# Two layers of a hybrid token mixer and MoE: norm and modulation in the transposed layout, projection by stream, alternating heads and halving sums

## The reference, cut

```
def trunk_layer(x, cvec, lw, gla_s0, k_ctx, v_ctx):
    sh1, sc1, g1, sh2, sc2, g2 = ada_mod(cvec, lw['w_ada'], lw['b_ada'])      # silu(c) @ w_ada + b_ada, in six
    h = rms_norm(x, lw['norm_mix']) * (1 + sc1) + sh1
    gq, gk, gv, gg, glr, conv_in, nq, nk, nv = jnp.split(h @ lw['w_in'], split_points, axis=-1)
    gla_o, gla_state = gla_mixer(...)                                         # gated linear attention, both directions
    conv_o = conv_module(...)
    na = attend_dense(q, k, v)  or  neighborhood_attention(q, k, v, k_ctx, v_ctx, lw['na_rpb'])
    mix = jnp.concatenate([gla_o, conv_o, from_heads(na)], axis=-1) @ lw['w_out']
    x = x + g1 * mix
    h = rms_norm(x, lw['norm_ffn']) * (1 + sc2) + sh2
    x = x + g2 * moe(h, ...)          # sigmoid router, top 8 of 64 experts within 4 of 8 groups, one shared expert
```

## Time and profile before

| | |
|---|---|
| median of 3 runs | 1586.37 us (1584.79 to 1589.13) |
| the profiled execution | 1593.01 us, its span 1591.3 us |
| mean granted TensorE clock | 0.966 of full |
| busy in the span | PE 92%, PEld 49%, DVE 29%, ACT 16%, POOL 7% |
| costliest group, expert matmuls L939 on `ring` | 375.4 us busy, 25.5 us of waits, 15.0 of them for loads |
| loads of expert weights | 3 x 128 of 1 MB, 14.8 to 17.2 us from issue to landing |

### The profile page before, as it was taken

The page is one execution under the profiler, slowest core; times in us unless marked ns, Lnnn a source line. Parts: engine busy times, 40 slices in busy tenths (PEclk is TensorE's granted clock), DMA queues, the critical chain, the costliest instruction groups (busy, mean ns, idle before and its releaser), DMA issues. The chain is left out here.

```text
span 1591.3 us, 28207 instructions
## 1 busy us (share of the span) xinstructions
PE 1463.2 (92%) x12120; PEld 781.4 (49%) x12121; DVE 459.7 (29%) x956; ACT 260.0 (16%) x441; POOL 107.1 (7%) x349
## 2 busy tenths in 40 slices
PE   4899989899999998999959999889999999999996
PEld 3665765644434443434436667564443444344442
DVE  2291784501111110111133639571111111111112
ACT  1223211511111110111113131041111111111110
POOL 2600430000000000000000016000000000000000
PEclk8999989899999999999989999989999999999999
DMA  7755960399999999999944678207999999999994
GB/s 252 257 181 190 334 218 1 134 421 420 421 421 406 400 422 397 421 420 420 374 158 137 245 260 309 87 1 327 421 420 416 421 421 420 419 400 421 419 421 178
DMA packets 109252, 509.56 MB, mean 320 GB/s; under 512 B 12864, under 2 KB 14652, under 8 KB 59196
## 3 DMA queue, kind: packets, MB, share of 16 engines
q1 hardware_dynamic: 108508, 506.52, 79.4%
q0 software_dynamic: 384, 1.05, 0.2%
q10 hardware_dynamic: 224, 0.06, 0.0%
HBM read 505.49 MB, written 2.10 MB: 319 GB/s over the span
## 5 line engine op out<-in xcount | busy, mean ns | idle before, releaser
L939 PE MATMUL ps<-ring,h 128*32 128x512 f32 x2720 | 375.4, 601 | 25.5 <-DMA ring<-in_exp_w_up 15.0
L939 PEld LDWEIGHTS ps<-ring,h 128*32 128x32 f32 x2720 | 110.3, 111 | 248.9 <-issue 248.9
L958 PE MATMUL ps<-ring,work 128*32 128x512 f32 x1360 | 199.6, 598 | 3.1 <-DVE store L1545 1.6
L939 PE MATMUL ps<-store,h 128*32 128x512 f32 x608 | 189.9, 615 | 9.0 <-issue 5.4
L965 PE MATMUL ps<-store,work 128*128 128x512 f32 x416 | 192.4, 605 | 1.6 <-DVE store L1553 1.6
L925 PEld LDWEIGHTS ps<-tm,work 128*128 128x128 bf16 x2496 | 144.4, 98 | 44.3 <-issue 43.1
L925 PE MATMUL ps<-tm,work 128*128 128x128 bf16 x2496 | 156.9, 219 | 0.3
L1543 DVE TENSOR_TENSOR work<-work,ps 128x256 f32<-128x256 f32 x52 | 21.9, 422 | 410.7 <-ACT work L1239 410.7
L965 PEld LDWEIGHTS ps<-store,work 128*128 128x128 f32 x416 | 74.7, 189 | 120.0 <-issue 116.5
L1545 DVE COPY store<-ps 128x512 f32<-128x512 f32 x52 | 36.0, 692 | 328.9 <-PE ps L958 328.9
L673 PE MATMUL ps<-ring,store 128*128 128x512 f32 (+1 forms) x256 | 101.3, 555 | 0.0
(11 more groups left out here) (276 smaller groups left out, 1316.8 us busy)
## 6 DMA issues: line engine op xcount, KB each, us to landing
ring<-in_exp_w_gate SPq DMA_DIRECT2D x102, 1024.0 KB, 15.0
ring<-in_exp_w_up SPq DMA_DIRECT2D x102, 1024.0 KB, 17.2
ring<-in_exp_w_down SPq DMA_DIRECT2D x102, 1024.0 KB, 15.5
ring<-in_w_ada SPq DMA_DIRECT2D x28, 2048.0 KB, 10.4
store<-in_exp_w_gate SPq DMA_DIRECT2D x26, 1024.0 KB, 15.0
store<-in_exp_w_up SPq DMA_DIRECT2D x26, 1024.0 KB, 17.1
work<-in_exp_w_down SPq DMA_DIRECT2D x26, 1024.0 KB, 14.8
ring<-in_w_in SPq DMA_DIRECT2D x6, 2048.0 KB, 13.0
```

Source lines behind the costliest of these rows:

```text
L939: last = mm(ps[first:first + TILE, 4, :], X_e[:, b, kt, first:first + TILE], gate_up(slot, kt), start=(kt == 0), stop=(kt == KT - 1))
L958: last = mm(ps[first:first + TILE, 7, :], turn[:, P * j + first:P * j + first + TILE], down(slot, j, half), start=(j == 0), stop=(j == 1))
```

## The change

*Norm and modulation.* `modulate` and `turn_h` go. `modulation(k, b)` puts scale and shift on the partitions of the transposed layout, channel by channel, with four products of 8 columns; the two norm gains come as 16 rows of 512 bytes and are transposed with them. VectorE makes a diagonal matrix of the inverse roots (`diagonal`), `turn_x` multiplies the tiles of `x` by it, which transposes and normalises, and `keep_hT` writes `hT` with scale and shift: the first four tiles on ScalarE, the other four on VectorE. The order of channels in `hT` changes, so that w_in, the router's weights and the shared gate and up are loaded with rows k * 128 + p on partition p. For the experts `hT` is turned back (`turn_back`), copied by ScalarE to `h_by_k` with the old order of channels, split there, and the rests are made on GpSimd.

*Projection.* The state's transposes go to banks 0 and 1, `mix(0, ...)` stands ahead of the states and `mix(1, ...)` behind; gates are shown before the head tiles and kept by ScalarE (`g1`); the head tiles of stream 0 come first, both halves, then stream 1. Squares, root, turn, logits follow stream by stream. The third split moves behind the copy of the tables on ScalarE, the expert order goes to bank 2.

*Linear attention.* `pairs` alternates the heads from matmul to matmul and waits once, until both heads of the group before are masked. The sums over levels are adds of halves.

```diff
+G1_BANKS = (4, 5, 0, 1)
+H_BANKS = ((3, 7), (4, 5))
...
+    g1 = [tmf[:, 0:512], tmf[:, 512:1024], hflat[:, 1024:1536], hflat[:, 1536:2048]]
...
-            eng.wait_ge(s["mix_shown"], 2 * (i + 1))
+            eng.wait_ge(s["mix_shown"], 3 + i)
...
-                           A["w_in"][layer, :, c0:c0 + cw].rearrange("(p k) n -> p k n", k=KT), sem)
+                           A["w_in"][layer, :, c0:c0 + cw].rearrange("(k p) n -> p k n", p=P), sem)
...
-            def modulation(k):
-
-                for st in range(STREAMS):
-                    for half in range(2):
-                        show(6 * k + 2 + half, st, 4 * st + half)
-                    for half in range(2):
-                        last = show(6 * k + half, st, 4 * st + 2 + half)
-                    last.then_inc(s["mod_shown"], 1)
-
-            def turn_h(k):
-                for st in range(STREAMS):
-                    pe.wait_ge(s["h_ready"], STREAMS * k + st + 1)
-                    ht = h[:, st, :].rearrange("t (p k) -> t k p", k=KT)
-                    for kt in range(KT):
-                        last = nc.tensor.transpose(bank(4 * st + kt // 4, P * (kt % 4), P * (kt % 4 + 1)),
-                                                   ht[:, kt, :], ident[:])
-                    last.then_inc(s["hT_shown"], 1)
+            def modulation(k, b):
+
+                if k == 0:
+                    pe.wait_ge(s["norm_in"], 32)
+                    nc.tensor.transpose(bank(b, 32, 32 + 2 * KT), gains, ident[0:2 * KT, 0:2 * KT])
+                for i, n in enumerate((6 * k + 2, 6 * k + 3, 6 * k, 6 * k + 1)):
+                    last = mm(bank(b, 8 * i, 8 * (i + 1)), ada[:, n, :], pick[:, :, :, 0], start=True, stop=True)
+                last.then_inc(s["mod_shown"], 1)
+
+            def turn_x(k, st):
+
+                pe.wait_ge(s["diag_ready"], STREAMS * k + st + 1)
+                for kt in range(KT):
+                    last = mm(bank(4 * st + kt // 4, P * (kt % 4), P * (kt % 4 + 1)), x[:, st, P * kt:P * (kt + 1)],
+                              diag[:, st, :], start=True, stop=True)
+                    if kt % 4 == 3:
+                        last.then_inc(s["hT_shown"], 1)
...
-                for e in range(2):
-                    if g:
-                        pe.wait_ge(s["masked"], 2 * (g - 1) + e + 1)
-                    r = slice(DK * e, DK * (e + 1))
-                    for lv in range(LEVELS + (dr == 0)):
+                if g:
+                    pe.wait_ge(s["masked"], 2 * g)
+                for lv in range(LEVELS + (dr == 0)):
+                    for e in range(2):
+                        r = slice(DK * e, DK * (e + 1))
                         out = bank((2, 6)[e] + lv // 4, P * (lv % 4), P * (lv % 4 + 1))
                         if lv < LEVELS:
                             last = mm(out, X[r, dr, lv, :], X[r, dr, lv, :], start=True, stop=True)
                         else:
                             last = mm(out, kT[r, a, P * st:P * (st + 1)], qT[r, a, P * st:P * (st + 1)],
                                       start=True, stop=True)
-                    last.then_inc(s["pair_shown"], 1)
+                        if lv == LEVELS - (dr != 0):
+                            last.then_inc(s["pair_shown"], 1)
...
-            pe.wait_ge(s["masked"], 16)
+            pe.wait_ge(s["E_ready"], 8)
             for a in range(PAIRS):
-                nc.tensor.transpose(bank(2, P * a, P * (a + 1)), kT[:, a, 0:P], ident[:])
+                nc.tensor.transpose(bank(0, P * a, P * (a + 1)), kT[:, a, 0:P], ident[:])
             for dr in range(2):
-                last = mm(bank(3, 256 * dr, 256 * (dr + 1)), suf[:, dr, :], la[:, 0, dr, :], start=True, stop=True)
+                last = mm(bank(1, 256 * dr, 256 * (dr + 1)), suf[:, dr, :], la[:, 0, dr, :], start=True, stop=True)
...
+            pe.wait_ge(s["masked"], 16)
+            pe.wait_ge(s["cat_conv"], 1)
+            pe.wait_ge(s["cat_na"], 1)
+            pre_loaded(pe, AT["out", 0])
+            for st in range(STREAMS):
+                mix(0, st, range(HEADS, KT))
+            pe.wait_ge(s["kd_ready"], 1)
+            for dr in range(2):
+                for hh in range(HEADS):
+                    last = mm(ps[0:DK, dr, DV * hh:DV * (hh + 1)], kd[:, dr, DK * hh:DK * (hh + 1)],
+                              v[:, 0, DV * hh:DV * (hh + 1)], start=True, stop=True)
+            last.then_inc(s["st_shown"], 1)
+            pre_loaded(pe, AT["out", 1])
+            for st in range(STREAMS):
+                mix(1, st, range(HEADS, KT))
+
+            pe.wait_ge(s["st_kept"], 1)
             for st in range(STREAMS):
                 pe.wait_ge(s["go_ready"], st + 1)
                 for hh in range(HEADS):
                     last = nc.tensor.transpose(bank(st, P * hh, P * (hh + 1)), gg[:, st, P * hh:P * (hh + 1)], ident[:])
                 last.then_inc(s["goT_shown"], 1)
-
             pe.wait_ge(s["bias_in"], 64)
-            pe.wait_ge(s["cat_gla"], STREAMS)
+            for st in range(STREAMS):
+                for half in range(2):
+                    if st == 1:
+                        pe.wait_ge(s["cat_gla"], half + 1)
+                    show(4 + half, st, G1_BANKS[2 * st + half]).then_inc(s["g1_shown"], 1)
             for half in range(2):
-                for st in range(STREAMS):
-                    show(4 + half, st, (4, 5, 0, 1)[2 * half + st])
-                    mix(half, st, range(HEADS)).then_inc(s["mix_shown"], 1)
-            pe.wait_ge(s["x_mid"], 4)
-            modulation(1)
-            turn_h(1)
-            pe.wait_ge(s["hT_ready"], 2 * STREAMS)
-
-            for st in range(STREAMS):
+                mix(half, 0, range(HEADS)).then_inc(s["mix_shown"], 1)
+            pe.wait_ge(s["g1_kept"], 1)
+            modulation(1, G1_BANKS[0])
+            for half in range(2):
+                mix(half, 1, range(HEADS)).then_inc(s["mix_shown"], 1)
+
+            def logits(st):
+                pe.wait_ge(s["hT_ready"], 2 * STREAMS + 2 * (st + 1))
                 for kt in range(KT):
                     last = mm(bank(2 + 4 * st, 0, EXPERTS), hT[:, kt, P * st:P * (st + 1)], wr[:, kt, :],
                               start=(kt == 0), stop=(kt == KT - 1))
                 last.then_inc(s["logits_shown"], 1)
+
+            def turn_back(st):
+                for kt in range(KT):
+                    last = nc.tensor.transpose(bank(H_BANKS[st][kt // 4], P * (kt % 4), P * (kt % 4 + 1)),
+                                               hT[:, kt, P * st:P * (st + 1)], ident[:])
+                last.then_inc(s["h_shown"], 1)
+
+            pe.wait_ge(s["g1_kept"], 4)
+            turn_x(1, 0)
+            logits(0)
+            pe.wait_ge(s["mod_ready"], 2)
+            turn_x(1, 1)
+            turn_back(0)
+            logits(1)
+            turn_back(1)
+            pe.wait_ge(s["h_copied"], 1)
...
+            def keep_hT(k, st):
+                act.wait_ge(s["hT_shown"], 2 * (STREAMS * k + st) + 1)
+                act.wait_ge(s["mod_ready"], k + 1)
+                for kt in range(KT // 2):
+                    last = nc.scalar.activation(hT[:, kt, P * st:P * (st + 1)], bank(4 * st, P * kt, P * (kt + 1)),
+                                                ACT.Identity, scale=mod_scale[:, kt, st:st + 1],
+                                                bias=mod_shift[:, kt, st:st + 1])
+                last.then_inc(s["hT_ready"], 1)
...
+            def squares(st, half):
+                act.wait_ge(s["x_mid"], 2 * st + half + 1)
+                u = 2 * st + half
+                nc.scalar.activation(g1[u], x[:, st, 512 * half:512 * (half + 1)], ACT.Square,
+                                     accum_out=half_ss[:, u:u + 1]).then_inc(s["square_done"], 1)
+
+            for half in range(2):
+                squares(0, half)
+            squares(1, 0)
+            keep_hT(1, 0)
+            squares(1, 1)
+            keep_hT(1, 1)
...
+            score(0)
+            copy_h(0)
+            score(1)
+            act.wait_ge(s["h_copied"], 1)
+            split_h(0, 0).then_inc(s["hs1"], 1)
+            copy_h(1)
+            act.wait_ge(s["h_copied"], 2)
+            split_h(0, 1).then_inc(s["hs1"], 1)
+            for st in range(STREAMS):
+                act.wait_ge(s["rest1"], st + 1)
+                split_h(1, st).then_inc(s["hs2"], 1)
...
-                    levels = tm[:, 0:n, :].rearrange("p l n -> p n l")
+                    link(tt(tm[:, 0:n - 4, :], tm[:, 0:n - 4, :], tm[:, 4:n, :], ALU.add))
+                    link(tt(tm[:, 0:2, :], tm[:, 0:2, :], tm[:, 2:4, :], ALU.add))
                     if dr == 0:
-                        link(nc.vector.tensor_reduce(att[:, a, e, :], levels, AX.X, ALU.add))
+                        link(tt(att[:, a, e, :], tm[:, 0, :], tm[:, 1, :], ALU.add))
                     else:
-                        link(nc.vector.tensor_reduce(att2[:, 0:P], levels, AX.X, ALU.add))
```

(29 more changed lines are left out.)

182 lines of the change are left out of this document (94 added, 88 removed).

## The result

The changed kernel takes 1566.03 us (median of 4 runs, 1564.86 to 1566.27) where the kernel before took 1587.75 beside it (1584.79 to 1591.06): ratio 0.986, 95% interval 0.984 to 0.988. Forecast were 1540 and a range from 1527 to 1557. Less than half of the gain is there. The profiled executions: span 1564.6 against 1591.3, 26.7 less instead of 46.5. That is more than the 21.7 between the medians, since the profiled execution of the kernel before, 1593.0, lies 5.3 above its median, and that of the changed one, 1566.3, only 0.2.

The account below looks back on a forecast made before the run. A fixed expert-weight stream behind a serial chain was taken as the bound. Gains at start, attention and tail, 25.3 us in layer 1 and 21.2 in layer 2, together 46.5, came off the 1586.4 median: 1540, range 1527 to 1557.

Parts of the forecast that it names:

- What bounds the kernel: Whole layer: a fixed expert-weight stream of some 490 us behind a serial part; each us off that part comes off the span.
- Start: Norm, modulation and transposition up to the projection: gain 6.0 us in layer 1 (5.2 plus 0.8 for the projection), 3.2 in layer 2.
- Two streams of 16 instructions at 0.116 = 3.7: Start, layer 1: the turn of x on TensorE was put at 3.7 us.
- Attention: Linear attention: two-group cycle 12.9 us instead of 14.45, VectorE becoming the bound; 6 us saved per layer.
- Less 0.6 where ScalarE's queue issues bias loads: Linear attention: 0.6 us of the saving lost where bias loads are issued ahead of an exponential.
- the halvings: Attention's level sums on VectorE: adds of halves at 1.52 us instead of 1.98; 1.8 and 2.0 allowed beside GpSimd.
- The rival of the shared port in the attention: Attention: two-input VectorE adds and GpSimd hold each other up; about 13.9 us a cycle, total 1546; chance 0.13.
- Tail to the scores: From the attention's end T to the router's scores: scores at T+52.3 us instead of T+66.3.
- The clock in the tail: Rival: TensorE's clock falls after gaps between T+41 and T+52; about +5 us per layer, total 1550; chance 0.13.
- Routing: From scores to first expert load: small VectorE operations run beside GpSimd, 1 us more; first load at T+65.2.
- GpSimd's subtractions: Rival: the chain before the first gather is slow; at 15 us each, 38 us per layer, total 1617; chance 0.02.
- the heads in the array: Rival: attention's heads do not alternate in the array; cycle 15.3 us, 3 slower per layer, total 1558; chance 0.06.

Follow-up runs that it names:

- experiment 5: Changed kernel with the first three k tiles of the shared gate and up behind the order's matmuls instead of in front: 1573.0 us, ratio 0.990.
- Experiment 6: Changed kernel with 16 idle identity matmuls on TensorE at the start of each layer, before the modulation: 1561.9 us, ratio 0.984.
- experiments 7 to 9: Changed kernel with level sums by tensor_reduce again (1565.8 us), with heads one after the other again (1575.8), and with both (1571.7).
- experiment 1: Changed kernel, but GpSimd starts its four subtractions only when the expert order is known, with ScalarE's copies moved ahead of its wait: 1544.7 us, ratio 0.973.
- experiment 2: Changed kernel with each of GpSimd's four subtractions made in eight pieces of 128 columns, at the same place: 1551.05 us, ratio 0.977.
- experiment 4: Changed kernel with 56 idle identity matmuls on TensorE between the g2 broadcasts and the counting, subtractions where they were: 1565.3 us, ratio 0.985.

## Why the prediction was wrong

**What bounds the kernel: right.** A fixed stream behind a serial part; what came off the serial part came off the span, once per layer. One refinement, from experiment 5 alone: the end of the serial part is the first gather, not the first load. With the gate and up where they are the two are 11.24 apart, so the sum could be made at either.

**Start: mechanism right, one term too small.** "Two streams of 16 instructions at 0.116 = 3.7" was 6.19 in layer 1. The price was a row of TensorE at full clock, and the change itself takes away the 64 instructions (8.80 us) that had brought the clock up before: 0.57 was granted from 36 to 40 us and 1.00 from 40 to 44, where the changed kernel has 0.50 from 36 to 46. Experiment 6 puts the clock back and gets 3.84 and 47.56. Gain 2.8 instead of 5.2; the projection behind it gained 1.5 (15.74 to 14.20) instead of 0.8. In layer 2 the low clock was in the sum: 4.1 gained, 3.2 forecast.

**Attention: right in size, wrong in its parts.** 4.9 instead of 6 (9.3 at the last level sum, less 2.8 and 1.5). Two heads run at once in the array as read from the scores' rows: 1.83 where 1.74 was worked out. VectorE became the bound, at 12.6 instead of 12.9. (The four adds of seven levels, put at 2.0, are 2.1 by their own terms, 1.73 and 0.1 for each; nothing hangs on it.) "Less 0.6 where ScalarE's queue issues bias loads" was 1.64. But the halvings, which the sum had in VectorE's loop, earned nothing net (experiments 7 to 9): the reduce would have been enough.

**The rival of the shared port in the attention** exists and is small there: 56 ns on each product, 0.8 a group, where 2.0 had been worked out, and with it one wait of 1.64.

**Tail to the scores: right.** T+51.3 for T+52.3; stream 0's heads done at T+31.9 (forecast T+33), stream 1 at T+39.7 (T+40.8). **The clock in the tail**, the second rival, came in the changed kernel's trace only once, in layer 2: the sixteen turn instructions of stream 1 in 3.63 instead of 1.95. That it stayed out of layer 1 is luck: in the experiments' traces, with the same code there, this turn takes 2.02 in six cases and 3.54 to 3.65 in the other six, experiment 1 among them, whose scores come 1.1 later though its first turn starts 0.6 earlier. What decides isn't shown.

**Routing: the step that failed.** "Routing's small VectorE operations now run beside GpSimd: 1 us more." It was 9.96 us per layer: 12.9 from the scores to the first load were forecast, 12.1 it had been, 22.1 it is. Experiment 1 takes away the overlap alone and gives 12.12, and 21 us come back in the total. Of the 26 missing there, 19.8 stand in the trace (26.7 for 46.5). The other 6.4 are no stage's: the gain was worked out on an execution of 1593.0 and taken off a median of 1586.4, as if the changed kernel's profiled execution would lie 6.6 above its median too, and it lay 0.2 above. What made the 1593.0 longer isn't shown. The parts: 7.0 in four VectorE operations, each of which stands while one subtraction runs (experiments 1 and 2), and 3.0 of low clock after the idle that this makes (experiment 4). The row that held the price was in the prediction: two additions of 256 columns took 1.84 beside a GpSimd operation of 1.40; 0.43 + 1.40 = 1.83, which, read with experiments 1 and 2, is one wait for that operation and not a slower pace. I read it for the attention, where GpSimd's operations are 0.33 long, and there I gave it 3 us and 0.13. In the routing GpSimd's operations are 2.1 long, back to back, beside a chain of short dependent operations: each link costs a whole GpSimd instruction. I had looked at these subtractions only for whether they end in time for the gather; they do, with room, and at 2.12 each instead of 2.8.

The Trainium skill has it (SBUF — State Buffer, Who interferes with whom): the port pair that VectorE and GpSimd share is an exclusive lock, held "for the whole instruction", and a VectorE instruction with two SBUF inputs runs into a GpSimd one that reads SBUF. At the routing the trace agrees: 2.10, 2.15, 2.21 against 2.12. The same section has tensor_reduce free of it and copies, casts and scalar operations in their two-port modes bound by it, which experiment 1's rows bear out (0.20; 2.05 and 2.02), as far as they can: the trace doesn't show an operation's mode.

**The account of layer 1:** forecast 25.3, measured 14.35. Missing: 1.7 at the start with the projection, 1.1 in the attention, 9.2 in the routing; the tail gave 1.0 more. **Layer 2:** forecast 21.2, measured 11.8. From the last issue of layer 1 to the last level sum 9.0 were gained (9.2 forecast), from there to the scores 12.9 (12.8), and the routing, 22.47 instead of 12.36, lost 10.1 (0.8).

**The range** was too narrow because of the routing alone: with the overlap taken away the kernel is at 1544.7, inside it. Of the four priced rivals none bore on the ranks: the port was priced in the attention, the clock up to the counting, the heads in the array, and GpSimd's subtractions only for the first gather, the wrong waiter.

## What to carry to other kernels

Before moving work to GpSimd, list VectorE's operations that will run beside it: each one that reads only SBUF (two inputs, or a scalar operation or cast with one) can cost the length of a whole GpSimd instruction, so the price is the number of links in the chain times that length. Put long GpSimd instructions where VectorE's results are not waited for, or cut them into pieces, which gives back less (14.66 from the scores to the first load against 12.12, and 22.08 uncut). A saved stretch of TensorE work may have been what kept its clock up: price what follows at the clock that the new idle time leaves.

## What the runs showed of the hardware

- Waiting is by whole instructions. Of four GpSimd instructions in 8.48 us, if they are of equal length, each was followed within 0.05 to 0.14 us by the end of one VectorE operation (270.91, 273.10, 275.24, 277.36), so that VectorE got one in between any two. In eighths an operation takes 0.1 to 0.3 longer than alone, and GpSimd's 32 pieces take 12.70, 0.40 each instead of 0.27.
- MAX8 (sixteen in 1.19 as before, the last 0.5 of it beside GpSimd), tensor_reduce and operations that read PSUM weren't held; a scalar operation and a cast of 64x64 from SBUF were, for 2 us each, as firmly as additions. Beside the pieces of experiment 2 one scalar operation was held (L1561, 0.48 instead of 0.20) and one wasn't (L1548, 0.23 as ever).
- Idle time of TensorE has a price behind it: after 8.03 us of it, six instructions of 512 columns took 4.78 instead of 2.84; filled with matmuls of the identity, 2.84 again, and all from the counting to the first load 3.0 shorter.
- Two matmuls in different halves of the array's rows start at once and cost as one: 28 instructions in 1.83 instead of 3.05.
